# Second block's joints: the last three units for the first token tile first, the third and fourth units of the next site split later, the last update in pieces, chunks 4 to 7 turned late

## What is computed

```python
def second_block(x, norm_gains, w_ffn_gate, w_ffn_up, w_ffn_down, w_in, w_out, ...):
    for layer in range(DEPTH):                       # 2
        g = norm_gains[layer]
        h = rmsnorm(x, g[0])
        x = x + 0.5 * rmsnorm(swiglu(h, w_ffn_gate[layer, 0], ...), g[1])
        h = rmsnorm(x, g[2])
        x = x + rmsnorm(token_mixer(h, w_in[layer], w_out[layer], ...), g[3])
        h = rmsnorm(x, g[4])
        x = x + 0.5 * rmsnorm(swiglu(h, w_ffn_gate[layer, 1], ...), g[5])
    return x
def swiglu(h, w_gate, w_up, w_down):                 # hidden width 2816
    return (jax.nn.silu(h @ w_gate) * (h @ w_up)) @ w_down
def rmsnorm(x, g):
    return x * rsqrt(mean(x * x) + 1e-6) * g
```

## Time and profile before

| | |
|---|---|
| median of 3 runs | 1436.45 us (1434.94 to 1437.26) |
| the profiled execution's own time | 1433.49 us |
| its span in the profile | 1431.7 us |
| TensorE (PE) busy | 98% of the span |
| VectorE (DVE) busy | 71% |
| ScalarE (ACT) busy | 51% |

### The profile page before, as it was taken

How to read it: one execution, slowest core, us unless ns; L and a number is a source line. 1 busy time by engine, 2 the same in 40 slices (tenths; PEclk the granted TensorE clock), 3 DMA queues, 4 the chain that set the end, 5 groups by cost and what they waited for, 6 DMA issues and landing times.

```text
span 1431.7 us, 22179 instructions
## 1 busy us (share of the span) xinstructions
PE 1397.8 (98%) x8063; PEld 1159.4 (81%) x8063; DVE 1018.2 (71%) x1693; ACT 726.8 (51%) x1244; POOL 73.2 (5%) x98
## 2 busy tenths in 40 slices
PE   5999999999999999999999999999999999999998
PEld 2768747869868888888888888888888888888887
DVE  2588455469677777787687777877777876877776
ACT  4433164345574444575664444654444756644444
POOL 0300211200110000000200000000000002000000
PEclk9999999999999999999999999999999999999999
DMA  9623184274235655764335565646655643455662
GB/s 356 194 88 89 59 289 171 89 223 142 95 133 174 196 188 176 250 182 139 118 133 176 177 202 193 204 152 202 202 177 178 195 143 119 133 176 178 203 200 94
DMA packets 185654, 243.03 MB, mean 170 GB/s; under 512 B 4560, under 2 KB 154608, under 8 KB 185456
## 3 DMA queue, kind: packets, MB, share of 16 engines
q1 hardware_dynamic: 182272, 229.43, 49.6%
q0 software_dynamic: 2736, 10.55, 2.1%
q10 hardware_dynamic: 576, 2.10, 0.4%
HBM read 241.01 MB, written 1.05 MB: 169 GB/s over the span
## 4 chain that ended last, share of the span: by engine, by line
PE 78%; DVE 8%; DMA 7%; ACT 4%; issue 3%; SPq 0%; POOL 0%; DVEq 0%; ACTq 0%; POOLq 0%
PE bank L1966 38%; PE bank L2485 16%; PE bank L2487 8%; DMA weight_ring<-in_w_ffn_up 3%; DVE weights_low L1562 2%; PE bank L2093 2%; ACT weights_high L981 2%; DMA weight_ring<-in_w_ada 2%; DMA weight_ring<-in_w_in 1%; PE bank L1947 1%; DMA weight_ring<-in_w_ffn_down 1%; PE bank L2313 1%; PE bank L2338 1%; DVE arena L1556 1%; DVE weight_ring_low L1242 1%
## 5 line engine op out<-in xcount | busy, mean ns | idle before, releaser
L1562 DVE TENSOR_TENSOR weights_low<-weight_ring,weights_high 128x1024 fp32r<-128x1024 f32 x328 | 393.3, 1223 | 125.6 <-ACT weights_high L981 125.4
L981 ACT ACTIVATE weights_high<-weight_ring 128x1024 fp32r<-128x1024 f32 x328 | 334.6, 1048 | 99.1 <-PE bank L1966 62.0
L2485 PE MATMUL bank<-input_split,weights_high 128*128 128x512 f32 x1280 | 319.5, 391 | 0.0
L2485 PEld LDWEIGHTS bank<-input_split,weights_high 128*128 128x128 f32 x1280 | 234.7, 188 | 45.0
L2487 PEld LDWEIGHTS bank<-input_split,weights_low 128*128 128x128 f32 x1280 | 174.6, 190 | 12.5
L2487 PE MATMUL bank<-input_split,weights_low 128*128 128x256 f32 x1280 | 178.5, 282 | 0.0
L1966 PE MATMUL bank<-weights_high,hidden_high 128*128 128x512 f32 x352 | 138.6, 394 | 1.4 <-DVE hidden_low L1671 1.4
L1055 ACT ACTIVATE silu_gate<-gate_sum 128x256 f32<-128x256 f32 x88 | 36.8, 418 | 203.3 <-DVE gate_sum L1649 200.3
L1966 PE MATMUL bank<-weights_low,hidden_high 128*128 128x512 f32 x352 | 137.9, 392 | 0.0
L1966 PE MATMUL bank<-weights_high,hidden_low 128*128 128x512 f32 x352 | 137.0, 389 | 0.0
L1966 PE MATMUL bank<-input_split,weights_high 128*128 128x256 f32 x576 | 105.6, 285 | 0.0
(11 more groups left out here) (353 smaller groups left out, 2251.7 us busy)
## 6 DMA issues: line engine op xcount, KB each, us to landing
weight_ring<-in_w_ffn_gate SPq DMA_DIRECT2D x44, 1024.0 KB, 5.3
weight_ring<-in_w_ffn_up SPq DMA_DIRECT2D x44, 1024.0 KB, 5.3
weight_ring<-in_w_ffn_down SPq DMA_DIRECT2D x44, 1024.0 KB, 4.9
weight_ring<-in_w_in SPq DMA_DIRECT2D x32, 1024.0 KB, 5.4
weight_ring<-in_w_ada SPq DMA_DIRECT2D x24, 1024.0 KB, 6.1
weight_ring<-in_w_out SPq DMA_DIRECT2D x16, 1024.0 KB, 5.1
weight_ring<-in_w_in SPq DMA_DIRECT2D x24, 512.0 KB, 4.7
gain_row<-in_norm_gains POOLq DMA_DIRECT2D x6, 512.0 KB, 3.8
```

The source lines that it names most:

```text
L981: A(unit_in(WH, U), unit_source(U), ACT.Copy).then_inc(s_high, 1)
L1562: TTn(unit_in(WL, U), unit_source(U), unit_in(WH, U).bitcast(F32), ALU.subtract).then_inc(s_low, 1)
L2485: mm(b[:, :].rearrange("p (h n) -> p h n", h=2), unit_in(WH, U)[:, k, :], HX[:, k, :, :], start=(k == 0), stop=False, skip_group_check=True)
```

## The change

On TensorE, the tail of each site now does all three row units for tile 0 (the first two units in both halves, then the third), and then for tile 1 half by half. The second filler of a joint has 256 columns instead of 512. Chunks 0 to 3 are turned for both tiles at once, and chunks 4 to 7 only inside `first_units`, after its third chunk. On ScalarE and VectorE, the third unit of the next site is split after tile 0's root and update, if the site that ends is an ffn; the fourth unit is split after the input copies (ffn to mix) or after the new scale is made (ffn to ffn). The split of an ffn's last unit moves ahead. The residual's update of tile 1 is made in 256, 256 and 512 columns, with the gain of the last half between (the last site keeps its order). The square of X's first half moves into `site_tail`. Joint 0, out of the first block, keeps its order. The core of the diff (line numbers of the changed file are higher by 5 to 36):

```diff
 # ScalarE, site_norm(i)
             if i:
-                x_square(i, 0, 0)
                 x_square(i, 0, 1)
-            if i and SITES[i - 1][0] == "ffn":
-                high(unit_base[i] + EARLY - 1)
             for c in range(KD):
...
+            if i and SITES[i - 1][0] == "ffn" and SITES[i][0] == "mix":
+                high(unit_base[i] + EARLY - 1)
             for hf in range(2):
                 x_square(i, 1, hf)
             act.wait_ge(*at("x_mean", "ready", i))
             A(stat[:, 8:10], stat[:, 6:8], ACT.Sqrt).then_inc(*done("rms_ready", "site", i))
+            if i and SITES[i - 1][0] == "ffn" and SITES[i][0] == "ffn":
+                high(unit_base[i] + EARLY - 1)
             high(unit_base[i] + 4)
 # ScalarE, site_tail(i)
+                        if t and i < 5:
+                            x_square(i + 1, 0, 0)
...
+                if t == 0 and i < 5 and SITES[i][0] == "ffn":
+                    high(unit_base[i + 1] + EARLY - 2)
 # VectorE, site_norm(i) and inverse(i)
-            if i == 0 or SITES[i - 1][0] == "ffn":
+            if i == 0 or SITES[i - 1][0] == "ffn" and SITES[i][0] == "mix":
                 low(unit_base[i] + EARLY - 1)
...
             last.then_inc(*done("norm_diag", i))
+            if i and SITES[i - 1][0] == "ffn" and SITES[i][0] == "ffn":
+                low(unit_base[i] + EARLY - 1)
 # VectorE, site_tail(i), new
+            update(0, 1, slice(512, 1024))
+            if i < 5 and SITES[i][0] == "ffn":
+                low(unit_base[i + 1] + EARLY - 2)
+            gained(1, 0)
...
+                scale(1)
+                update(1, 0, slice(0, 256), "first")
+                update(1, 0, slice(256, 512))
+                gained(1, 1)
+            update(1, 1, slice(512, 1024))
 # TensorE, site_norm(i)
             turned(0, (0, 1, 2, 3))
+            if i:
+                warm(1, 256)
+                turned(1, (0, 1, 2, 3))
+                return lambda: (turned(0, (4, 6)), turned(1, (4, 6)), turned(0, (5, 7)), turned(1, (5, 7)))
 # TensorE, first_units
+                if c == 2:
+                    rest_turned()
 # TensorE, end of mix
-            out_rows(5)
-            for t in range(2):
+            for ks in ((5, 6), (7,)):
                 for hf in range(2):
-                    out_rows(6, (t,), (hf,))
-                    out_rows(7, (t,), (hf,))
+                    for k in ks:
+                        out_rows(k, (0,), (hf,))
+            for hf in range(2):
+                for k in (5, 6, 7):
+                    out_rows(k, (1,), (hf,))
```

More of the change, by code:

```diff
@@ L1104, in ffn @@
                 high(a + 5)
+                high(a + 6)
                 hidden_high(1, f + 2, None, to=2)
-                high(a + 6)
-                for U in ahead[1:]:
+                for U in ahead[1:2]:
                     high(U)
@@ L1723, in ffn @@
                 TTn(hbuf[:, 1, :], B[3][:, 0:T], sgate[:, 1, :], ALU.mult).then_inc(s_h, 1)
-                low(a + 5)
+                low(a + 6)
                 hidden_low(1, f + 2, to=2)
-                low(a + 6)
-                for U in ahead[1:]:
+                for U in ahead[1:2]:
                     low(U)
@@ L2424, in site_norm, with warm @@
             def site_norm(i):
-                def warm(count):
+                def warm(count, width=512):
                     for _ in range(count):
-                        mm(B[0][:, :], ident, KB[:, 0:512], start=True, stop=True)
+                        mm(B[0][:, 0:width], ident, KB[:, 0:width], start=True, stop=True)
                 def turned(t, chunks):
@@ L2434, in turned @@
                                 pe.wait_ge(*at(*r))
-                        pe.wait_ge(*(at("x_new", i - 1, t, c // 4) if i else at("final_scaled", t, c // 4)))
+                        if i == 0:
+                            pe.wait_ge(*at("final_scaled", t, c // 4))
+                        elif t and c < 2:
+                            pe.wait_ge(*at("x_new", i - 1, 1, 0, "first"))
+                        else:
+                            pe.wait_ge(*at("x_new", i - 1, t, c // 4))
                         last = tr(B[X_BANK[c]][:, half * T + t * P:half * T + (t + 1) * P], X[:, t, c * P:(c + 1) * P], ident)
@@ L2488, in wide_product, with ffn @@
                 return last
-            def ffn(i, n):
+            def ffn(i, n, rest_turned):
                 f0 = n * FFN_CHUNKS
@@ L2682, in mix @@
                         pe.wait_ge(*at(*r))
-                first_units(i, u0, [B[PB2[key]] for key in firsts], 0)
+                first_units(i, u0, [B[PB2[key]] for key in firsts], 0, rest_turned)
                 norm_sum(i)
@@ L2749, in _ @@
             for i, (kind, n) in enumerate(SITES):
-                site_norm(i)
-                (ffn if kind == "ffn" else mix)(i, n)
+                (ffn if kind == "ffn" else mix)(i, n, site_norm(i))
 INPUTS = ["x", "c", "ctx", "c_ctx", "w_ada", "w_in", "w_uq", "w_ukv", "w_pw", "w_fourier", "sgu_ln_g", "sgu_ln_b", "w_s", "b_s",
```

52 lines of the change are left out of this document (30 added, 22 removed).

## The result

The changed kernel takes 1451.31 us, the median of six runs (1449.66 to 1454.84); the kernel before took 1436.67 beside it (six runs, 1434.94 to 1439.71). The ratio is 1.011, 95% interval 1.0098 to 1.0122: slower by 14.6 us, where I had forecast slower by 9.5, and 0.8 us above my range. The profiled execution took 1450.23 us, span 1448.0, which is 16.3 us more span than before.

The account below looks back on a forecast made before the run. PE, 98% busy, was taken as the bound, so time is won only in its fillers or waits. 2 x 3.8 + 2.2 + 0.7 - 1.0 = +9.5 on 1436.45 gave 1446.0 us, range 1441.5 to 1450.5.

Parts of the forecast that it names:

- Joints 2 and 5: the used count: At joints 2 and 5, ScalarE's last mix split waits for a later count and delays y's squares: +3.8 us each.
- the 0.1 that I had in place of 3.60: At joints 2 and 5, the new order with nothing in its way: first unit plus transposes 3.7 in place of 3.60.
- Joint 3: the fourth unit and its slot: At joint 3, the later fourth split delays the up weights' load and PE's down projection: +2.2 us.
- the upper end that I had named for a mean that is not sooner: At joint 3, the cost if the mean is not sooner: 2.8 us.
- Joints 1 and 4: Fourth split delays norm_sum to 10.7 us after the filler's start: joint 4 +0.7; joint 1, squaring y sooner, -1.0.
- The rest: Site 5's tail after its last matmul and the sooner split of an ffn's last unit: 0.
- rival C: At joints 2 and 5, PE's idling drops the clock to 1.2 GHz: up to +5.8 us a joint, 8% chance.
- the sign that the prediction itself had named for being wrong: Behind joints 2 and 5, the clock row falling below 1.00 would show the forecast wrong overall.

Follow-up runs that it names:

- e2: The changed kernel with filler matmuls of 512 columns added in the waits of joints 2 and 5; 1447.42 us, ratio 1.0091 to the kernel before.
- e4: The kernel before with one part of the change alone, the new tail of the mix sites; 1442.73 us, ratio 1.006.
- e1: The changed kernel with the old tail of the mix sites put back; 1441.38 us, ratio 1.0051 to the kernel before.
- e7: The changed kernel, new tails kept, with the fourth split of every joint behind the last root and ahead of the input copies; 1437.98 us, ratio 1.0016.
- e9: The changed kernel with the fillers of e2 and five more filler calls ahead of site 3's first down projection; 1446.68 us, ratio 1.0073.
- e3: The changed kernel with joint 3's fourth split put back ahead of the input copies on ScalarE; 1447.86 us, ratio 1.0093 to the kernel before.
- e6: e5 with the fourth split ahead of the input copies at joints 1 and 4 too; 1437.47 us, ratio 1.0009 to the kernel before.
- e12: The kernel before with only the third unit split behind the first root of y at joint 1; 1435.22 us, ratio 0.9995.
- e5: The changed kernel with the edits of e1 and e3 together; 1438.36 us, ratio 1.0014 to the kernel before.
- e8: e6 with the short filler and the late turn of chunks 4 to 7 only out of an ffn; 1437.11 us, ratio 1.0008.
- e10: The kernel before with joint 1's third unit split behind the first root of y and three fillers in joint 0's wait; 1432.99 us, ratio 0.9977.
- e11: The kernel before with only three more fillers at joint 0; 1434.59 us, ratio 0.9997.

## Why the prediction was wrong

The direction and each of the waits that I had worked out were right. The median came out 14.6 us above before, not 9.5.

**Joints 2 and 5: the used count.** Right in place and size: +3.8 each predicted; +3.99 each with the clock kept up (e2), +3.52 with the old joint (e4). The split starts at E-1.1, as predicted, the first unit at E+6.69 with the clock up (e2; predicted 6.5), E+6.84 with the fallen clock. The new joint alone costs 0.45 out of a mix (e1), not the 0.1 that I had in place of 3.60. Putting the split elsewhere takes all but 0.6 of it back at each joint with the new order of products kept (e7).

**Joint 3: the fourth unit and its slot.** Right in place: DMA at E+11.4 (predicted 11.05), its 5.29 us as before, a wait of 2.84 us, PE at E+18.74 (predicted 18.2). The cost of the wait was sized at +2.2; E to the down projection grew by 2.81, the upper end that I had named for a mean that is not sooner: the split of a+3 starts at E+9.05, SyncE issues 0.33 later than predicted, and the 0.26 from hidden_low's end to PE's start (951.04 to 951.30) was missing in my sum. Behind it the 12 matmuls took 4.13 in place of 2.79, 1.3 us more; in e9, with the clock at 1.00, they took 3.16, so 1.0 of the 1.3 is the clock by that row. Site 3 and joint 3 together are +4.16. With the split put back (e3) they are +0.60.

**Joints 1 and 4.** Signs right: +0.98 (predicted +0.7), -0.54 (predicted -1.0). Norm_sum at joint 1 stands at 11.20, not 10.7, and in e6 at 10.96 while joint 4 has 10.50; that the two joints differ I have not followed to its end.

**The rest.** Predicted 0. Site 5's tail is unchanged, as said. But joint 0, which the diff does not touch, is +1.37 in this profile, by the clock alone, and the remaining stretches come to less than 0.1 net.

**The step that failed is the clock, which the sum priced at nothing**: rival C, "the clock falls on top", had 8% and only the upper end of the range. I turned it down from one place, joint 0, where a wait of 2.06 us had left the clock at 1.00, and took that as a property of such a wait. That row is the stretch of the wait itself and could not have shown a fall behind it: in the changed kernel the same stretch also reads 1.00, and the fall comes in the next.

```profile
422.00:424.00 2.00, 0.66 (x5) 0.36 (x3) 1.91 (x4) 1.71 (x6) 0.00 (x0) 1.00 0.03 10
```

In the profile of before the clock did stay up behind the wait as well, but that was one draw. Twelve profiles have that wait in place (before, after, e1 to e9, e12), and in seven of them the clock fell behind it (after, e3, e4, e5, e8, e9, e12), at 1.35 to 1.53 us a time. In the changed kernel the clock was down at joint 2, at joint 5, in site 3's wait and at joint 0. The terms that I had sized came, on the joints and sites they name, to 3.99 x 2 + 2.81 + 0.98 - 0.54 = +11.2 without the clock. The other 5.1 of the 16.3 are 2.12 and 0.18 at joints 2 and 5, 1.35 in site 3, 1.37 at joint 0, and less than 0.1 net elsewhere. So of the miss of 6.8 on the profiled span, 5.0 is the clock (4.7 if 0.4 of site 3 is something else) and 1.7 the sizes. The 1.37 of joint 0 is no effect of the change: the one profile of before happened to have no fall there, about half of its runs have one. That share drops out of the difference of the medians, where the miss is 5.1: 1.7 the sizes, and 3.4 left for the falls at joints 2 and 5 and in site 3, which come to 3.65 in the profile. Without any clock my sum with the measured sizes would be 1436.45 + 11.2 = 1447.7 us, inside the range. The fall behind joints 2 and 5 was the sign that the prediction itself had named for being wrong.

I priced C at up to +5.8 a joint, as if the clock stayed down until all of first_units was done. It came back sooner, after 3.4 or 6.8 us, and only the part that lies over weight work costs: 4.4 us of it for 2.12 (joint 2), 3.6 for 1.79 (joint 5 of e3, 5.78 less 3.99), none for 0.18 (joint 5), 3.4 at joint 0, transposes included, for 1.35 to 1.53. That is 0.4 to 0.5 us for each us at the lower level amid such work, by these rows.

The Trainium skill, "TensorE: Matmul & The Clock Gate", Part 1, says that an idle TensorE goes back to half clock, and that the point at which the clock rises again differs from run to run of the same kernel. The traces agree that it goes to half, and they show more than the page says: here it differed between executions whether the clock fell at all. What the page says of the rise was reason enough not to rest on one trace, and I had passed over it.

**What stays open.** Which joint falls in a given execution. The wait of 2.40 was followed by a fall at joints 2 and 5 of the changed kernel and of e3, four of four, and at neither joint of e4; 2.06 at joint 0 in seven of twelve. The second wait is ruled out as the cause, as each fall came before it. PE's rows up to the fall at joint 5 (a wait, then transposes) are of the same kind as e4's, so it may be chance or the moment at which a wait comes; no run here sets that moment, and neither is shown. It also stays open why the clock was down for 3.4 us at some places and 6.8 at others, and how often each happens: there is one profile of each kernel. Site 3 still had +0.5 to +1.5 in e3, e5 and e6. A wait of 0.3 for hidden_low ahead of the first down projection stayed in all three; e5 and e6 have another 0.3 near the site's end for a late weights_low, and the rest I have not followed. Site 2 shows what single profiles do by chance: its longest wait for a hidden_low, at E+41 to E+47, is 0.43 us in before and 1.20 in e12, whose code is the same there. And the part of e10's gain that its halves don't have.

## What to carry to other kernels

When products are reordered, ask of every count that they raise when it now comes true, and go through each in-order queue that waits for it: here the last split of a mix stood ahead of the squares of y and moved with the count, for 4 us a joint; behind the last root of y the same split cost 0.6. When a split is moved later, follow the slot that it frees: the load that waits for it was the longest way in the joint. And an idle TensorE costs its wait and then, some of the time, the clock behind it (0.2 to 2.1 us a time here, by how much weight work stood in the low stretch), so price a wait of two microseconds or more with both, look at more than one execution before ruling the second out, and put fillers into a wait that can't be removed, sized from their own row so that they end inside it.

## What the runs showed of the hardware that was not expected

One and the same wait (2.06 us at joint 0, PE busy before and behind it) left the granted clock at 1.00 in some executions and dropped it to 0.50 in others. A wait of 2.40 us was followed by a fall in four places of six, three times with the clock down for 6.8 us and once for 3.4, PE being busy 99 to 100% of the stretches from 744 to 748 at 0.50. Each of these falls came 0.1 to 1.0 us after PE was back at work. With fillers (matmuls on constants) in the wait the granted clock stayed at 1.00 in all seven places that had them (joints 2 and 5 in e2 and e9, site 3 in e9, joint 0 in e10 and e11), and e9, which does 2.6 us more work at each of two joints and 4.4 in site 3, was faster than the changed kernel.
